# One half of the second layer's input weights stays on chip between the token tiles; the weights' ring has three places instead of four, the gathered rows' ring eight instead of ten

## The chip, the cores and the metric

The kernel runs on one core of a Trainium2 chip. The metric is the device time of one execution in microseconds (us). The median of three runs of the kernel before is 1578.97 us (1577.9 to 1581.96).

## What is computed

A decoder trunk of two layers on 256 tokens of width 1024, all in float32. Layer 0 mixes the tokens with gated linear attention, layer 1 with differential softmax attention. Each layer ends in an expert retrieval (PEER): every token picks 16 experts in each of 8 heads and takes a dot product with each expert's `u` row and a weighted sum of the `v` rows. Cut to what matters here:

```
for i in range(2):
    hn = rmsnorm(h, norm_mix[i])
    h = h + (gla_mixer if i == 0 else diff_mixer)(hn, ...)   # diff: proj = hn @ w_in (1024 x 3072), attention, @ w_out
    h = h + peer(rmsnorm(h, norm_ffn[i]), w_query[i], sub_keys[i], expert_u[i], expert_v[i])
...
def peer(...):             # per block of 128 tokens
    qry = x_blk @ w_query                                    # 1024 x 2048
    idx, gate = top 16 of the product keys, softmax          # 8 heads x 16 experts a token
    act = gelu(einsum('thkd,td->thk', expert_u[idx], x_blk))
    return einsum('thk,thkd->td', gate * act, expert_v[idx])
```

## The kernel before

**Tiles and rows.** The 256 tokens are two tiles of 128 (one token a partition). Each layer and tile has 128 expert slots, so there are 4 x 128 = 512 "rows" in all, numbered n = 0 to 511: rows 0 to 255 belong to layer 0, 256 to 383 to layer 1's first tile, 384 to 511 to its second. A row is one indirect DMA from POOL's queue: for each of the 128 partitions, the `u` and `v` vector of one expert, 8 KB a partition, 1 MB in all. DVE takes the dot product with `u` (`dot`), ACT makes gelu, weight and a 128x128 diagonal matrix of the weights (`expert_weight`), and PE multiplies that matrix with `v` into PSUM (`expert_sum`, two 128x512 products, four MATMUL records a row). PE's last product of a row counts up `v_used`. Eleven of the early rows are summed by DVE instead.

**The ring of gathered rows.** A gathered row lands in one of several places of 8 KB a partition. From row 128 on these are the ten of `LATE`; row n waits until row n - 10 is summed (`v_used`). So at any moment the ten places are split between rows on their way and rows that have landed and are not yet summed.

**Ticks.** The rest of the work (queries, attention, searches) is laid between the rows by hand: each engine's program calls `at(t)`, which emits the row work up to tick t, one row a tick. On PE the products of layer 1 (`block1`, `query1`) stand between the sums of the rows; all of it is one stream in a fixed order.

**Layer 1 for one tile** (`layer1(m)`, m = 0 and 1, starting at ticks 134 and 262): six blocks of the input projection (`block1`), attention in eight heads (`diff`), two blocks of the output projection (`block1`), four blocks of the PEER query (`query1`). While layer 1 of a tile is worked, the rows of the tile before are summed.

**The weights' ring.** The weights of these 12 blocks (2 MB each) come as 24 halves of 1 MB for each tile, in order: halves 0 to 11 are `diff_in`, 12 to 15 `diff_out`, 16 to 23 the query's. They are loaded by SP's queue into four places `A_HALF`; half n waits until half n - 4 is used. `block1` uses its two halves one after the other and counts up `half_used` after each. `query1` is different: it needs both halves at its start, since each group of 128 outputs runs over all eight k, and it counts both as used at its end:

```
for j in range(2):
    pe.wait_ge(S(f"half_loaded{(halves + j) % 4}"), 16 * ((halves + j) // 4 + 1))
for g in range(4):
    for k in range(KD):
        at(t + Q_STEP * (KD * g + k + 1))
...
last.then_inc(S("half_used"), 2)
```

The wait stands ahead of the first `at`, so every row sum that follows in PE's program stands behind it.

Of the kernel before, what the change touches and what calls it, by code (L numbers as in the profile page):

```python
# [18 lines left out]
P = 128  # L19
D = 1024  # L20
KD = D // P
SEQ = 256
NT = SEQ // P
# [64 lines left out]
WBLK = KD * 512  # L88
# [6 lines left out]
A_PA = A_TI  # L95

A_HALF = (0, 2048, 16384, 18432)
A_GAIN, A_DV, A_KT, A_KEYT1, A_FINAL = 22528, 26624, 28672, 30720, 30720

ROW = 2 * D  # L100
FIRST = ("spare", "raw0", "raw1", 6144, 4096)
EARLY = ("work0", "work1", "spare", "raw0", "raw1", 6144, 4096, "work2", "work3")
LATE = (8192, 10240, 12288, 14336, 20480, "spare", "raw0", "raw1", 6144, 4096)


def homes():

    home, turn, before, last, used = [], [], [], {}, {}
    for n in range(ROWS):
# [4 lines left out]
        else:  # L114
            at = LATE[(n - SLOTS) % len(LATE)]
        home.append(at)
# [6 lines left out]
HOME, TURNS, BEFORE = homes()  # L123
ADDED = [n for n in range(16, 80, 6)]
SUMMED = [n for n in range(ROWS) if n not in ADDED]


def summed_to(n):
    return sum(k <= n for k in SUMMED)

# [6 lines left out]
def trunk_kernel(nc, x, x_t, gains_t, positions, norm_ffn, norm_final,  # L137
# [7 lines left out]
    with ctx:  # L145
        def sb(name, shape, dt=f32):
            return ctx.enter_context(nc.sbuf_tensor(name, shape, dt))
# [3 lines left out]
        def S(name):  # L151

            if name not in sems:
                sems[name] = ctx.enter_context(nc.semaphore(name))
            return sems[name]
# [19 lines left out]
        spare = sb("spare", [P, ROW])  # L175
        bank_all = ctx.enter_context(nc.psum_tensor("banks", [P, 8 * BANK], f32))

        def bank(b, n=1):
            return bank_all[:, b * BANK:(b + n) * BANK]

        def ar(off, n):
            return arena[:, off:off + n]
# [13 lines left out]
        def x1(unit, off=0, n=D):  # L196

            return work[:, unit * D + off:unit * D + off + n]
# [35 lines left out]
        @block.sync  # L234
        def _(sp):
            for m in range(NT):
                sp.dma_start(h[:, m, :], x[0, m * P:(m + 1) * P, :]).then_inc(S(f"x{m}_loaded"), 16)
            sp.dma_start(hnT[:].rearrange("p m k t -> p (m k t)"), x_t).then_inc(S("xt_loaded"), 16)
            for half, loaded in ((0, "win_top_loaded"), (1, "win_bottom_loaded")):
                c0 = half * WBLK // 2  # L240
                sp.dma_start(ar(c0, WBLK // 2), gla_in[0][:, c0:c0 + WBLK // 2]).then_inc(S(loaded), 16)
            for j, lq in enumerate((lq1, lk1, lq2, lk2)):
                sp.dma_start(rt[:, 256 + 64 * j:256 + 64 * j + DDH], lq.broadcast_to([P, DDH])
                             ).then_inc(S("lam_loaded"), 16)

            sp.wait_ge(S("gate_done"), 1)
            sp.dma_start(hrows[:, 1, :], norm_ffn[0].rearrange("(a n) -> a n", a=1).broadcast_to([P, D])
                         ).then_inc(S("gffn_loaded"), 16)
            sp.dma_start(ar(A_KEYT, HP * P), peer_keys_t[0]).then_inc(S("keys_loaded"), 16)
            for blk in range(4):  # L250
                sp.wait_ge(S(("v_done", "r_done")[blk // 2]), NT + blk % 2 + 1)
                sp.dma_start(ar(A_WQ + blk * WBLK, WBLK), peer_query[0, blk]).then_inc(S(f"wq_loaded{blk}"), 16)

            sp.wait_ge(S("scores_done"), 4 * NT)
            sp.dma_start(ar(A_KEYT1, HP * P), peer_keys_t[1]).then_inc(S("keys1_loaded"), 16)
            sp.dma_start(ar(A_GAIN, D), norm_ffn[1].rearrange("(a n) -> a n", a=1).broadcast_to([P, D])
                         ).then_inc(S("gffn1_loaded"), 16)

            def load_halves(m, first, w, blocks):

                for j in range(2 * blocks):
                    n = 24 * m + first + j
                    if n == 0:
                        sp.wait_ge(S("listed"), NT * LISTS)
                    elif n > 3:
                        sp.wait_ge(S("half_used"), n - 3)
                    c0 = j % 2 * WBLK // 2
                    sp.dma_start(ar(A_HALF[n % 4], WBLK // 2), w[j // 2][:, c0:c0 + WBLK // 2]
                                 ).then_inc(S(f"half_loaded{n % 4}"), 16)

            for m in range(NT):
                load_halves(m, 0, diff_in, 6)
                load_halves(m, 12, diff_out, 2)
                load_halves(m, 16, peer_query[1], 4)

            sp.wait_ge(S("ffn1_rows"), NT)
            sp.dma_start(ar(A_GAIN, D), norm_final.rearrange("(a n) -> a n", a=1).broadcast_to([P, D])
                         ).then_inc(S("gfinal_loaded"), 16)
            sp.wait_ge(S("out_ready"), 1)
            sp.dma_start(out[0, 0:P, :], ar(A_FINAL, D)).then_inc(S("out_stored"), 16)  # L280
            sp.wait_ge(S("out_ready"), 2)
            sp.dma_start(out[0, P:2 * P, 0:512], ar(A_FINAL + D, 512)).then_inc(S("out_stored"), 16)
            sp.wait_ge(S("out_stored"), 16 * 2)
            sp.wait_ge(S("last_stored"), 16)
# [61 lines left out]
        def _(pe):  # L346
# [196 lines left out]
            def at(t):  # L543

                nonlocal summed
                while summed < ROWS and SUM_T[summed] < int(t):
                    if summed not in ADDED:
                        expert_sum(summed)
                    summed += 1

            halves = 0

            def block1(t, dst):

                nonlocal halves
                for k in range(KD):
                    at(t + IN_STEP * (k + 1))
                    if k % (KD // 2) == 0:
                        pe.wait_ge(S(f"half_loaded{halves % 4}"), 16 * (halves // 4 + 1))
                    last = nc.tensor.matmul(dst, x1(X_T, k * P, P),  # L560
                                            ar(A_HALF[halves % 4] + k % (KD // 2) * 512, 512),
                                            start=(k == 0), stop=(k == KD - 1))
                    if k % (KD // 2) == KD // 2 - 1:
                        last.then_inc(S("half_used"), 1)
                        halves += 1
# [55 lines left out]
            def layer1(m):  # L621
# [9 lines left out]
                for b in range(6):  # L631
                    if b == 4:
                        at(t + IN_END[3])
                        pe.wait_ge(S("rope_ready"), 2 * m + 1)
                        turn(x1(X_Q), 6, "q_turned")
                    if b > 3:
                        pe.wait_ge(S("in1_evicted"), 6 * m + b - 1)
                    block1(t + IN_END[b] - KD * IN_STEP, bank((6, 7, 4, 5, 4, 5)[b]))
# [13 lines left out]
                for b in range(2):  # L652
                    block1(t + OUT_END[b] - KD * IN_STEP, bank(4 + b))
# [5 lines left out]
                for b in range(4):  # L659
                    query1(m, b, t + Q_END[b] - 4 * KD * Q_STEP)  # L660
# [3 lines left out]
            def scores1(m, b):  # L664
                pe.wait_ge(S("keys1_loaded"), 16)
                pe.wait_ge(S("qry1_evicted"), 4 * m + b + 1)
                for g in range(4 * b, 4 * b + 4):
                    last = nc.tensor.matmul(bank(4 + b)[:, g % 4 * P:(g % 4 + 1) * P], x1(X_QRY, g * P, P),
                                            ar(A_KEYT1 + g * P, P), start=True, stop=True)
                last.then_inc(S("scores1_done"), 1)  # L670

            def query1(m, b, t):

                nonlocal halves
                for j in range(2):
                    pe.wait_ge(S(f"half_loaded{(halves + j) % 4}"), 16 * ((halves + j) // 4 + 1))
                for g in range(4):
                    for k in range(KD):
                        at(t + Q_STEP * (KD * g + k + 1))
                        w = A_HALF[(halves + k // (KD // 2)) % 4] + k % (KD // 2) * 512 + g * P  # L680
                        last = nc.tensor.matmul(bank(4 + b)[:, g * P:(g + 1) * P], ar(w, P), x1(X_T, k * P, P),  # L681
                                                start=(k == 0), stop=(k == KD - 1))
                    if g == 0 and b:
                        scores1(m, b - 1)
                last.then_inc(S("half_used"), 2)
                halves += 2
# [1042 lines left out]
```

## Time and profile before

| | us |
|---|---|
| median of three runs | 1578.97 |
| the profiled execution | 1579.55 |
| its span | 1577.5 |
| PE busy | 1362.1 (86%) |
| DVE busy | 975.1 (62%) |
| ACT busy | 670.4 (42%) |
| POOL busy | 580.3 (37%) |
| moved by DMA | 620.42 MB, mean 393 GB/s |

The time of an execution lies some 2 us over its span. The lines of a page name an engine, a source line of the kernel and the operation; PE's busy time is modelled and includes pipelined matmuls, DMA has its own share and rate. Times on the trace's axis count from the span's start.

### The profile page before, as it was taken

Reading aid. Unit: us, or ns where it says so; the run is one execution under the profiler, and the core shown is the slowest. Engines: PE = TensorE matmul, PEld = TensorE weight load, DVE = VectorE, ACT = ScalarE, POOL = GpSimd, SP = SyncE. Lnnn points to the kernel's source line nnn. Section 1 sums busy time; section 2 is a strip of 40 time slices with the busy share of each in tenths; the row PEclk is TensorE's granted clock in tenths of the full one; section 3 lists DMA queues with packets and bytes.
Section 4 is the critical chain, followed back from the end, with each engine's and each line's share of the span. In section 5 each row is a group of like instructions: output and inputs, shape, how many; then the busy total and the mean of one; then the engine's idle time right before and its main releaser. Section 6 shows DMA issues by size and latency. Waiting matters only on the chain.

```text
span 1577.5 us, 15019 instructions
## 1 busy us (share of the span) xinstructions
PE 1362.1 (86%) x4096; PEld 656.8 (42%) x4096; DVE 975.1 (62%) x2432; ACT 670.4 (42%) x1914; POOL 580.3 (37%) x532
## 2 busy tenths in 40 slices
PE   7999998889877988889989699888999877787776
PEld 5555565444323433334555244334465422222222
DVE  3327598988774344764477765566556888554544
ACT  2324443434334334873434333586433434443433
POOL 1001565554443333443433234334434433333330
PEclk9999999999998999999999799999999999999999
DMA  9317999999999999999999999999999999999995
GB/s 380 146 54 293 396 413 421 421 421 421 421 421 422 421 421 421 421 421 421 421 421 421 372 422 421 421 413 399 421 421 420 421 421 421 422 422 422 421 421 230
DMA packets 85234, 620.42 MB, mean 393 GB/s; under 512 B 10368, under 2 KB 10368, under 8 KB 11424
## 3 DMA queue, kind: packets, MB, share of 16 engines
q0 software_dynamic: 74768, 551.65, 84.4%
q1 hardware_dynamic: 9792, 67.51, 10.5%
q8 instruction: 34, 0.56, 0.1%
q10 hardware_dynamic: 592, 0.31, 0.1%
q14 instruction: 48, 0.39, 0.1%
HBM read 618.38 MB, written 1.05 MB: 393 GB/s over the span
## 4 chain that ended last, share of the span: by engine, by line
PE 40%; DMA 37%; DVE 9%; ACT 9%; issue 4%; POOL 1%; SPq 0%; ACTq 0%; DVEq 0%; POOLq 0%
PE banks L533 25%; DMA arena<-in_peer_uv_dram,hnT 24%; PE banks L560 6%; PE banks L413 5%; DMA work<-in_peer_uv_dram,hnT 5%; DMA raw<-in_peer_uv_dram,hnT 4%; DVE arena L1413 3%; DMA rt<-in_diff_lambda_k_dram 2%; ACT g_e L917 2%; PE banks L681 2%; DMA spare<-in_peer_uv_dram,hnT 2%; ACT L954 1%; PE banks L505 1%; ACT hnT L909 1%; DVE raw L1413 1%
## 5 line engine op out<-in xcount | busy, mean ns | idle before, releaser
L533 PE MATMUL banks<-arena,g_e 128*128 128x512 f32 x1184 | 585.1, 622 | 116.1 <-ACT g_e L917 115.0
L339 POOL DMA_INDIRECT arena<-in_peer_uv_dram,hnT x299 | 326.3, 1091 | 515.8 <-PE banks L533 497.8
L533 PEld LDWEIGHTS banks<-arena,g_e 128*128 128x128 f32 x1184 | 214.3, 195 | 405.5 <-ACT g_e L917 213.2
L906 ACT ACTIVATE hnT<-hnT 128x1 f32<-128x1 f32 x512 | 103.3, 202 | 631.5 <-DVE hnT L1413 629.6
L1413 DVE CUSTOM_DVE_ANT_0 arena<-arena,hrows 128x1024 f32<-128x1024 f32 x209 | 254.2, 1223 | 170.2 <-DMA arena<-in_peer_uv_dram,hnT 168.9
L533 PE MATMUL banks<-raw,g_e 128*128 128x512 f32 x424 | 205.5, 611 | 27.8 <-ACT g_e L917 25.3
L917 ACT ACTIVATE g_e<-ident,hnT 128x128 f32<-128x128 f32 x501 | 201.2, 402 | 46.5 <-ACT hnT L909 0.7
L339 POOL DMA_INDIRECT raw<-in_peer_uv_dram,hnT x106 | 118.3, 1116 | 154.1 <-PE banks L533 149.5
L909 ACT ACTIVATE hnT<-hnT,arena 128x1 f32<-128x1 f32 x512 | 150.7, 294 | 52.1 <-DVE arena L1594 5.5
L1413 DVE CUSTOM_DVE_ANT_0 arena<-arena,banks 128x1024 f32<-128x1024 f32 x90 | 109.7, 1220 | 87.3 <-DMA arena<-in_peer_uv_dram,hnT 87.2
L1413 DVE CUSTOM_DVE_ANT_0 raw<-raw,hrows 128x1024 f32<-128x1024 f32 x80 | 97.6, 1224 | 57.2 <-DMA raw<-in_peer_uv_dram,hnT 56.3
L339 POOL DMA_INDIRECT spare<-in_peer_uv_dram,hnT x53 | 56.7, 1071 | 206.6 <-DVE hnT L1582 116.2
L533 PEld LDWEIGHTS banks<-raw,g_e 128*128 128x128 f32 x424 | 75.1, 192 | 123.8 <-issue 67.9
L560 PE MATMUL banks<-arena,work 128*128 128x512 f32 x256 | 124.1, 593 | 2.5 <-ACT work L939 2.5
L533 PE MATMUL banks<-work,g_e 128*128 128x512 f32 x200 | 98.8, 620 | 18.3 <-ACT g_e L917 16.3
L533 PE MATMUL banks<-spare,g_e 128*128 128x512 f32 x196 | 98.0, 624 | 9.6 <-ACT g_e L917 9.5
L339 POOL DMA_INDIRECT work<-in_peer_uv_dram,hnT x54 | 72.7, 1347 | 81.6 <-PE banks L533 41.6
L681 PEld LDWEIGHTS banks<-work,arena 128*128 128x128 f32 x512 | 70.1, 192 | 37.9 <-issue 37.9
L1413 DVE CUSTOM_DVE_ANT_0 work<-work,hrows 128x1024 f32<-128x1024 f32 x54 | 65.7, 1221 | 24.4 <-DMA work<-in_peer_uv_dram,hnT 23.4
L505 PEld LDWEIGHTS banks<-arena 128*128 128x128 f32 x448 | 61.9, 191 | 34.9 <-issue 34.9
L560 PEld LDWEIGHTS banks<-arena,work 128*128 128x128 f32 x256 | 48.5, 190 | 64.4 <-issue 60.3
L681 PE MATMUL banks<-work,arena 128*128 128x128 f32 x512 | 70.7, 275 | 0.0
(244 smaller groups left out, 1259.2 us busy)
## 6 DMA issues: line engine op xcount, KB each, us to landing
arena<-in_diff_in_dram SPq DMA_DIRECT2D x24, 1024.0 KB
arena<-in_peer_query_dram SPq DMA_DIRECT2D x16, 1024.0 KB
arena<-in_gla_in_dram POOLq DMA_DIRECT2D x5, 2048.0 KB, 20.3
arena<-in_peer_query_dram SPq DMA_DIRECT2D x4, 2048.0 KB, 10.9
arena<-in_diff_out_dram SPq DMA_DIRECT2D x8, 1024.0 KB
arena<-in_peer_uv_dram,hnT POOLq DMA_INDIRECT x299
work<-in_gla_out_dram POOLq DMA_DIRECT2D x2, 2048.0 KB, 40.0
arena<-in_gla_in_dram SPq DMA_DIRECT2D x2, 1024.0 KB, 12.3
```

What stands on the lines that cost most here:

```text
L339: pool.indirect_dma_start(pair(n), None, table, bass.IndirectOffsetOnAxis(ap=places[:, o:o + 1].bitcast(u32), axis=0)).then_inc(S(f"pair_l ...
L413: last = nc.tensor.matmul(dst, hnT[:, m, k, :], w[:, k * 512:(k + 1) * 512], start=(k == 0), stop=(k == KD - 1))
L505: last = nc.tensor.matmul(dst[:, g * P:(g + 1) * P], ar(A_WQ + b * WBLK + k * 512 + g * P, P), ar(A_HN + m * D + k * P, P), start=(k == 0) ...
L533: last = nc.tensor.matmul(bank(2 * (tile % NT) + half), diags[:, slot * P:(slot + 1) * P], v_row(n)[:, half * 512:(half + 1) * 512], start ...
L560: last = nc.tensor.matmul(dst, x1(X_T, k * P, P), ar(A_HALF[halves % 4] + k % (KD // 2) * 512, 512), start=(k == 0), stop=(k == KD - 1))
L681: last = nc.tensor.matmul(bank(4 + b)[:, g * P:(g + 1) * P], ar(w, P), x1(X_T, k * P, P), start=(k == 0), stop=(k == KD - 1))
L906: A(acts[:, o:o + 1], dots[:, o:o + 1], ACT.Gelu).then_inc(S("gelu_done"), 1)
L909: A(weights[:, o:o + 1], acts[:, o:o + 1], ACT.Copy, scale=ar(A_GG + o, 1)).then_inc(S("weighted"), 1)
L917: A(diags[:, turn % DIAGS * P:(turn % DIAGS + 1) * P], ident[:], ACT.Copy, scale=weights[:, o:o + 1]).then_inc(S("diag_ready"), 1)
L954: last = A(x1(X_P, n % 2 * 512 + half * 256, w), x1(X_S, n % 2 * 512 + half * 256, w), ACT.Exp, bias=stat[:, 52 + (n % 2) * 2 + half:53 + ...
L1413: V.tensor_tensor_reduce(out=u_row(n), in0=u_row(n), in1=normed, scale=1.0, scalar=0.0, op0=ALU.mult, op1=ALU.add, accum_out=dots[:, o:o + ...
```

## The change

Half 5 of each tile's 24 (the second half of the third input block) gets a place of its own, 18432, the former fourth place of the ring. It is loaded in the first tile and not again in the second. All other halves go round three places: 0, 2048 and 16384. `RING` lists them; a half waits for the one three before it in that list. `LATE` loses two of its ten places, 14336 and 20480; nothing else in layer 1 takes them. No instruction of PE, DVE or ACT is added, removed or moved.

```diff
+KEPT = {5: 18432}
+HALVES = 24
+RING = [n for n in range(NT * HALVES) if n % HALVES not in KEPT]
...
-LATE = (8192, 10240, 12288, 14336, 20480, "spare", "raw0", "raw1", 6144, 4096)
+LATE = (8192, 10240, 12288, "spare", "raw0", "raw1", 6144, 4096)
...
+def half_at(n):
+
+    if n % HALVES in KEPT:
+        return KEPT[n % HALVES]
+    return A_HALF[RING.index(n) % 3]
+
+
+def half_turn(n):
+
+    return 0 if n % HALVES in KEPT else RING.index(n) // 3
...
-                    n = 24 * m + first + j
+                    n = HALVES * m + first + j
                     if n == 0:
                         sp.wait_ge(S("listed"), NT * LISTS)
-                    elif n > 3:
-                        sp.wait_ge(S("half_used"), n - 3)
+                    if n % HALVES in KEPT and m:
+                        continue
+                    if n in RING[3:]:
+                        sp.wait_ge(S("half_used"), RING[RING.index(n) - 3] + 1)
                     c0 = j % 2 * WBLK // 2
-                    sp.dma_start(ar(A_HALF[n % 4], WBLK // 2), w[j // 2][:, c0:c0 + WBLK // 2]
-                                 ).then_inc(S(f"half_loaded{n % 4}"), 16)
+                    sp.dma_start(ar(half_at(n), WBLK // 2), w[j // 2][:, c0:c0 + WBLK // 2]
+                                 ).then_inc(S(f"half_loaded_{half_at(n)}"), 16)
...
                 for j in range(2):
-                    pe.wait_ge(S(f"half_loaded{(halves + j) % 4}"), 16 * ((halves + j) // 4 + 1))
+                    pe.wait_ge(S(f"half_loaded_{half_at(halves + j)}"), 16 * (half_turn(halves + j) + 1))
```

On SP's queue, the loads of the halves stood so before (the row's number of repeats is behind the x, what it waits for in brackets):

```order
L268 DMA arena<-in_diff_in_dram 128x2048 [waits listed]
L268 DMA arena<-in_diff_in_dram 128x2048 x3
L268 DMA arena<-in_diff_in_dram 128x2048 [waits half_used] x8
L268 DMA arena<-in_diff_out_dram 128x2048 [waits half_used] x4
L268 DMA arena<-in_peer_query_dram 128x2048 [waits half_used] x8
L268 DMA arena<-in_diff_in_dram 128x2048 [waits half_used] x12
```

and stand so now, at another line number:

```order
L285 DMA arena<-in_diff_in_dram 128x2048 [waits listed]
L285 DMA arena<-in_diff_in_dram 128x2048 x2
L285 DMA arena<-in_diff_in_dram 128x2048 [waits half_used] x2
L285 DMA arena<-in_diff_in_dram 128x2048
L285 DMA arena<-in_diff_in_dram 128x2048 [waits half_used] x6
L285 DMA arena<-in_diff_out_dram 128x2048 [waits half_used] x4
L285 DMA arena<-in_peer_query_dram 128x2048 [waits half_used] x8
L285 DMA arena<-in_diff_in_dram 128x2048 [waits half_used] x11
```

Three halves instead of four go out at once at the start, half 5 follows half 4 without a wait, and the second tile loads 11 halves of `diff_in` instead of 12. On POOL's queue, the gathers from row 127 on stood so before:

```order
L339 DMA arena<-in_peer_uv_dram,hnT 128x2048 [waits v_used]
L339 DMA arena<-in_peer_uv_dram,hnT 128x2048 [waits scores_done,listed]
L339 DMA arena<-in_peer_uv_dram,hnT 128x2048 x4
L339 DMA spare<-in_peer_uv_dram,hnT 128x2048 [waits v_used]
L339 DMA raw<-in_peer_uv_dram,hnT 128x2048 [waits v_used] x2
L339 DMA arena<-in_peer_uv_dram,hnT 128x2048 [waits v_used] x7
```

and stand so now:

```order
L356 DMA arena<-in_peer_uv_dram,hnT 128x2048 [waits v_used]
L356 DMA arena<-in_peer_uv_dram,hnT 128x2048 [waits scores_done,listed]
L356 DMA arena<-in_peer_uv_dram,hnT 128x2048 x2
L356 DMA spare<-in_peer_uv_dram,hnT 128x2048 [waits v_used]
L356 DMA raw<-in_peer_uv_dram,hnT 128x2048 [waits v_used] x2
L356 DMA arena<-in_peer_uv_dram,hnT 128x2048 [waits v_used] x5
```

A round of the ring is `spare`, two of `raw` and, now, five of `arena` instead of seven.

## Rows read from the trace of the kernel before

**Rows 1.** The page: DMA's share and rate in 40 slices of 39.4 us

```profile
DMA  9317999999999999999999999999999999999995
GB/s 380 146 54 293 396 413 421 421 421 421 421 421 422 421 421 421 421 421 421 421 421 421 372 422 421 421 413 399 421 421 420 421 421 421 422 422 422 421 421 230
```

**Rows 2.** Who waited for whom, 1250 to 1550 us, POOL: total, times, longest

```profile
POOL arena L339 <- PE banks L533: 132.1, 83, 7.9
POOL raw L339 <- PE banks L533: 37.6, 24, 3.6
```

**Rows 3.** Gathers issued (L339) from 0 to a time, xcount

```profile
0.00:748.80 748.80, 273.56 (x224) 0.98 0.91 377
0.00:890.00 890.00, 320.20 (x268) 0.97 0.93 383
0.00:1140.00 1140.00, 416.56 (x352) 0.97 0.94 389
0.00:1240.00 1240.00, 458.61 (x390) 0.97 0.95 392
```

**Rows 4.** DVE's records of dot products (L1413), two a row, from 0 to a time

```profile
0.00:748.80 748.80, 264.76 (x432) 0.98 0.91 377
0.00:890.00 890.00, 321.45 (x524) 0.97 0.93 383
0.00:1140.00 1140.00, 424.12 (x694) 0.97 0.94 389
0.00:1240.00 1240.00, 467.27 (x764) 0.97 0.95 392
```

**Rows 5.** Windows: us, PE, PEld, DVE, ACT, POOL busy (xcount), PEclk, DMA share, GB/s

```profile
748.80:773.40 24.60, 23.38 (x102) 14.37 (x101) 12.79 (x23) 11.53 (x33) 10.99 (x11) 1.00 1.02 422
774.90:801.60 26.70, 24.33 (x111) 15.26 (x110) 16.67 (x54) 8.69 (x28) 8.69 (x10) 1.00 1.01 421
801.60:830.30 28.70, 24.61 (x110) 15.24 (x109) 18.97 (x45) 9.06 (x29) 10.34 (x10) 1.00 1.01 422
831.90:861.20 29.30, 26.27 (x110) 15.98 (x109) 20.69 (x66) 12.31 (x33) 9.15 (x10) 0.94 1.01 421
1164.10:1187.80 23.70, 23.70 (x111) 15.05 (x110) 14.75 (x54) 7.86 (x27) 8.71 (x10) 1.00 1.01 420
1187.80:1215.10 27.30, 24.23 (x109) 14.97 (x108) 17.39 (x42) 8.96 (x28) 9.94 (x9) 1.00 1.02 422
1216.90:1241.10 24.20, 23.90 (x110) 15.11 (x109) 20.61 (x66) 12.20 (x33) 11.37 (x11) 1.00 1.01 421
```

**Rows 6.** SP's issues in order of time around the end of a query block

```profile
773.42 29.02 SPq L268 DMA_DIRECT2D arena<-in_peer_query_dram  x4
```

**Rows 7.** SP's issue of one half at 719.23, and DMA queues 719.2 to 728.2

```profile
719.23 0.33 SPq L268 DMA_DIRECT2D arena<-in_peer_query_dram  x1
q1 hardware_dynamic: 144, 1.05, 28.0%
```

**Rows 8.** A load of 1 MB at the program's start: KB, us to landing

```profile
hnT<-in_x_t_dram SPq DMA_DIRECT2D x1, 1024.0 KB, 7.2
```

**Rows 9.** POOL's gathers in order of time, 875 to 900 us, idle before in brackets

```profile
875.80 1.66 POOL L339 DMA_INDIRECT arena<-in_peer_uv_dram,hnT  x1 [4.67 <-PE banks L533]
890.16 0.94 POOL L339 DMA_INDIRECT arena<-in_peer_uv_dram,hnT  x1 [12.71 <-PE banks L533]
```

**Rows 10.** Windows of 5 us at the drain, columns as in rows 5

```profile
885.00:890.00 5.00, 3.89 (x6) 1.71 (x7) 5.00 (x23) 2.56 (x9) 0.00 (x0) 0.50 0.85 354
890.00:895.00 5.00, 5.00 (x17) 2.94 (x16) 5.00 (x20) 3.29 (x13) 1.88 (x2) 0.90 0.72 261
```

**Rows 11.** PE in order of time at the same place

```profile
886.11 3.78 PE L533 MATMUL banks<-arena,g_e 128*128 128x512 f32 x4 [10.58 <-ACT g_e L917]
```

**Rows 12.** Windows around the second tile's attention, columns as in rows 5

```profile
1060.00:1085.00 25.00, 20.38 (x61) 9.26 (x59) 15.30 (x40) 21.60 (x65) 12.76 (x12) 1.00 0.96 372
1085.00:1140.00 55.00, 50.46 (x122) 23.11 (x123) 28.89 (x54) 24.14 (x75) 20.89 (x18) 0.94 1.01 422
```

More of the change, by code:

```diff
@@ L558, in block1 @@
                     if k % (KD // 2) == 0:
-                        pe.wait_ge(S(f"half_loaded{halves % 4}"), 16 * (halves // 4 + 1))
+                        pe.wait_ge(S(f"half_loaded_{half_at(halves)}"), 16 * (half_turn(halves) + 1))
                     last = nc.tensor.matmul(dst, x1(X_T, k * P, P),
-                                            ar(A_HALF[halves % 4] + k % (KD // 2) * 512, 512),
+                                            ar(half_at(halves) + k % (KD // 2) * 512, 512),
                                             start=(k == 0), stop=(k == KD - 1))
@@ L679, in query1 @@
                         at(t + Q_STEP * (KD * g + k + 1))
-                        w = A_HALF[(halves + k // (KD // 2)) % 4] + k % (KD // 2) * 512 + g * P
+                        w = half_at(halves + k // (KD // 2)) + k % (KD // 2) * 512 + g * P
                         last = nc.tensor.matmul(bank(4 + b)[:, g * P:(g + 1) * P], ar(w, P), x1(X_T, k * P, P),
```

## The prediction

> **What bounds the kernel now.** I read DMA's rate over the span first. From the sixth of the 40 slices on it is 421 GB/s in nearly every one [rows 1]. The dips are slice 23 (372) and slices 27 and 28 (413, 399). A rate that stays at one number while the work around it changes is a ceiling, so from about 200 us on the kernel lives at DMA's pace: a row or a half is 1.049 MB, and 1.049 MB at 421 GB/s is 2.49 us. Next, the waits of POOL, which issues the gathers. It waits for PE's sums nearly always (83 waits, 132.1 us, for the `arena` places alone in 300 us [rows 2]). That doesn't mean that PE is the bound: it means that the ring is always full, of rows on their way or landed. How they divide is what counts. Gathers issued less rows dotted (half of DVE's records) gives the rows on their way, with those landed and waiting for DVE: at 748.8 us 224 - 216 = 8, at 890 us 268 - 262 = 6, at 1140 us 352 - 347 = 5, at 1240 us 390 - 382 = 8 [rows 3, 4]. At 5 the rate is still 422 [rows 12]; where it dips (261 at 890 to 895 [rows 10], 372 at 1060 to 1085 [rows 12]) the reserve is gone. Four to five rows on their way fill the queues, so ten places hold a reserve of three to four rows in quiet stretches, none at 890, and hardly any at 1140. Last, PE in the query blocks. Where it lags (1164.1 to 1187.8) it is busy 23.70 us of 23.7 while DMA also runs at 420; the first tile's blocks are longer and have gaps [rows 5]. PE is thus the second bound, close behind.
>
> **What is taken away.** One load of 1 MB in the second tile, between 890 and 1000 us, where DMA is at its ceiling: -2.5 us.
>
> **The gathers' ring, eight places.** Row n now waits for row n - 8, so two rows fewer are on their way at each moment. In quiet stretches 8 become 6 and nothing is lost. Where the reserve runs out, DMA idles up to two rows longer, 2 x 2.49 = 5.0 us each time; the floor is 0. Three places come in question. (a) At 875 to 890 us POOL waits 12.71 us [rows 9] and the rate falls to 261 [rows 10]: no reserve is left, so I take the whole 5.0. (b) Before 725 us, in the first tile's attention, the rate holds at 421 through those slices [rows 1]; I take 1, of 0 to 5. (c) At 1060 to 1085 DMA idles already, but the engines are behind it, and PE is at 50.46 of 55.00 us in what follows [rows 12]. Rows that land later are not missed by an engine that is itself late: 0, of 0 to 5.
>
> **The weights' ring, three places.** Follow the half that a block waits for. `block1` uses a half each 8 us or so, and a half is now sent for when the third before it is used, two halves of time ahead (about 16 us); a load takes 9 (below), so these blocks don't wait. `query1` frees two halves together, at its end. In the first tile the query's halves are 16 to 23. In `RING`, half 19 waits for half 16, and 16 is freed only when query block 0 ends. But block 1 needs 18 and 19 before its first product. With four places half 19 waited for half 15, long done. So after block 0 PE stands until half 19 has been asked for and has landed. Half 20 goes out beside it; half 21 waits for 18, so block 2 waits the same way, and with half 23 block 3 too. Three stalls a tile, six in all. The kept half doesn't help: it is an input half, and far from here.
>
> How long is one? SP issues at the block's end (773.42, with its partner [rows 6]; the four issues of that row fall into two pairs, 28 us apart). A single half that was issued at 719.23 beside the gathers had its 1.05 MB moved, with the small writes that report it, by 728.2 [rows 7]: 9.0 us. At the program's start, with no gathers, 1 MB took 7.2 [rows 8]. So 7.2 to about 10, and I take 9.0, since the gathers are there. The Trainium skill says in "DMA: Bandwidth & Descriptors", section "Queues, rings and completion order", that each DMA engine takes turns between the queues that have work; by that rule a half gets half of the rate, 1.049 MB at 210 GB/s is an estimated 5 us of transfer, and what is left of the 9.0 is start and report. The trace agrees, and shows no way for the half to overtake.
>
> Behind the wait stand all of PE's row sums, so no place is freed meanwhile: POOL waits, ACT waits for the key scores of the block before, and DVE runs on with what has landed. What matters is whether PE makes good. A block's work for PE is at most 23.7 us (the row in which it was busy throughout), where the ones before took 26.7, 28.7 and 29.3 in the first tile and 23.7, 27.3 and 24.2 in the second [rows 5].
> - First tile: 3 x 9.0 = 27.0 of stall; spare 3.0 + 5.0 + 5.6 = 13.6; left 13.4. The ring enters with 8 - 2 = 6 on their way, a reserve of 1.5 rows over 4.5, 3.7 us: DMA loses 9.7.
> - Second tile: 27.0 less 0 + 3.6 + 0.5 = 4.1 leaves 22.9. Here the ring enters with no reserve. But before, the ring refilled to 8 by 1240; now it ends at 4.5 of 8 instead of 6, which DMA has kept working by 1.5 rows, 3.7 us. It loses 19.2.
> After 1240 there is only row work, DMA-bound, and what DMA lost isn't given back.
>
> **Sum.** -2.5 + 5.0 + 1 + 0 + 9.7 + 19.2 = +32.4 us. On the profiled execution's 1579.55 that is 1612; it lies 0.6 over the median, so I say 1612 and 2.1% slower.
>
> **Rivals.**
> - *The stalls are mostly covered* (0.18). The reserve of the ring and the gaps in PE take them, as a half is faster when the gathers run dry (7.2 each: 43.2 us less 17.7 of spare, less 7.4 of reserve: 18.1), and the second tile's blocks turn out to have more slack than their busy time tells. With the drain, 1583 to 1599. For it: PE's busy time is modelled. Against it: the row of 23.70 of 23.7 with DMA at 420.
> - *PE also comes back at a lower clock* (0.14). After the wait of 10.58 us PE's first four products took 3.78 us at a granted clock of 0.50 and the next window shows 0.90, one of its 5 us still low [rows 10, 11]; 0.50 is the lower of the two levels, 1.2 GHz. From 886.1 to 891 is 4.9 us, which at half speed costs 2.5; six times 2.5 is 15 more: 1620 to 1640. Against it: that low clock began in a stretch where PE had been idling between rows. "TensorE: Matmul & The Clock Gate" of the Trainium skill, section "HAM oscillation", says that a matmul loop which waits for its weights each time comes back cold each time. The trace has one such wait and it agrees; none lies in a busy query block.
> - *Not slower* (0.08): only the byte count matters, -2.5 us, 1577. It needs each stall and drain to be under the reserve: six rows on their way must outlast 9 us of standing PE, which two landed rows and a half use up once but not three times. It decides if a half is there within some 4 us of its issue.
> - *The change saves more than its bytes* (0.02), as SP's and POOL's traffic mingle less; no row speaks for it.
> - My forecast, stalls exposed at full clock (0.58): 1600 to 1626 as its own range.
>
> **How the numbers follow.** The own range and the two slow rivals reach from 1583 to 1640. Cutting the rare ends leaves 1588 to 1630, about 8 in 10. Within 0.3% (4.7 us, about what a measurement of this kernel can tell) is 1574.3 to 1583.7: the not-slower rival and the lowest edge of the covered one, 0.09. Faster 0.02, slower 0.89.
>
> **What would show it.** In the trace after: PE idle for 8 to 10 us at the starts of query blocks 1, 2 and 3 of each tile, ended by the landing of a half, six places in all, and none in `block1`. DMA's rate under 421 in the slices of both query stages (it was 421 in the first before), and deeper dips at 890. 1 MB less moved (619.4 MB). From the last query block to the end the same 2.49 us a row as before. Gathers issued less rows dotted at 6 in quiet stretches, where it was 8. It is wrong if PE's waits for the halves are short (then the load is faster than I read it), if they are there and DMA stays at 421 (then the reserve was larger), or if the rate falls in quiet stretches too (then six rows on their way don't fill the queues, and the time is beyond my range).

## The result and the profile after

The changed kernel takes 1614.56 us (median of 4, 1609.6 to 1616.25), the kernel before 1578.72. The ratio is 1.0222, 95% interval 1.0208 to 1.0236: 2.2% slower, 35 us. The profiled execution took 1616.25 us, its span is 1614.3, the span before was 1577.5. To compare runs of different calls, every difference below is a kernel's ratio to the kernel before that ran beside it, times 1578.7 us.

From the page of the changed kernel, PE's granted clock in 40 slices of 40.4 us, DMA's share and rate in the same slices, and what it moved:

```profile
PEclk9999999999998999999888999989988899999999
DMA  9317999999999999999988999999998899999996
GB/s 383 131 52 293 396 422 420 421 421 422 420 421 405 422 421 421 413 419 422 387 334 353 418 421 421 418 352 417 421 400 324 343 423 420 422 421 422 421 422 264
DMA packets 85090, 619.37 MB, mean 384 GB/s; under 512 B 10352, under 2 KB 10352, under 8 KB 11408
```

Where the kernel before held 421 [rows 1], there are now two valleys: slices 20 to 22 (387, 334, 353) and slices 30 to 32 (400, 324, 343). They are the two query stages. The granted clock reads 8 in just these six slices and in slices 13 and 27, 9 in all others. Slice 27, in the second tile's attention, is deeper than any was there before (352, where the lowest was 399), and at the first tile's end, where before slice 23 read 372, no dip is left: it reads 418 now. After slice 32 the rate is 421 again.

PE in order of time at the six places (start, us busy, line, operation, in brackets the idle time before and what ended it):

```profile
782.63 3.69 PE L550 MATMUL banks<-arena,g_e 128*128 128x512 f32 x4 [9.15 <-issue]
...
787.05 1.88 PE L550 MATMUL banks<-arena,g_e 128*128 128x512 f32 x4
...
819.18 1.20 PE L698 MATMUL banks<-work,arena 128*128 128x128 f32 x4 [9.38 <-DMA arena<-in_peer_query_dram]
...
854.65 2.90 PE L550 MATMUL banks<-spare,g_e 128*128 128x512 f32 x3 [9.54 <-issue]
...
1183.62 3.75 PE L550 MATMUL banks<-arena,g_e 128*128 128x512 f32 x4 [9.20 <-issue]
...
1221.80 1.19 PE L698 MATMUL banks<-work,arena 128*128 128x128 f32 x4 [10.15 <-DMA arena<-in_peer_query_dram]
...
1257.09 1.19 PE L550 MATMUL banks<-spare,g_e 128*128 128x512 f32 x1 [9.28 <-issue]
```

Leaving out the row at 787.05, these are the six stalls, 9.15 to 10.15 us, at the starts of query blocks 1, 2 and 3 of each tile. Two of the rows name the landing of the query's weights. The other four say "issue": the first instruction behind the wait is there a row sum (L550), which waits for nothing itself. I read them as the same wait: it stands alone ahead of an instruction, and what was late is known from the program's order. A row's four products took 3.69 us right after the first stall, and 1.88 at 787.05, which is the usual.

How POOL felt one of them, after the second stall:

```profile
824.07 1.62 POOL L356 DMA_INDIRECT arena<-in_peer_uv_dram,hnT  x1 [13.49 <-PE banks L550]
826.46 0.94 POOL L356 DMA_INDIRECT spare<-in_peer_uv_dram,hnT  x1 [0.77 <-PE banks L550]
```

Gathers issued (L356) from the start to a time, xcount:

```profile
0.00:749.50 749.50, 260.25 (x222) 0.98 0.91 374
0.00:824.00 824.00, 281.79 (x242) 0.97 0.91 375
0.00:1174.40 1174.40, 413.85 (x360) 0.96 0.93 382
```

and DVE's records of dot products (L1430), two a row:

```profile
0.00:749.50 749.50, 264.44 (x432) 0.98 0.91 374
0.00:824.00 824.00, 295.58 (x483) 0.97 0.91 375
0.00:1174.40 1174.40, 433.12 (x708) 0.96 0.93 382
```

On their way are 222 - 216 = 6 at 749.5, where it was 8 [rows 3, 4]; 242 - 241.5, at most one, at 824.0, just before POOL issues again behind the second stall; and 360 - 354 = 6 at 1174.4, where the second tile's stalls begin.

Windows over the changed kernel (us, PE, PEld, DVE, ACT and POOL busy with counts, granted clock, DMA share, GB/s):

```profile
740.00:885.00 145.00, 113.11 (x469) 68.11 (x468) 83.76 (x222) 50.98 (x151) 48.47 (x44) 0.89 0.93 369
885.00:1140.00 255.00, 228.31 (x582) 101.41 (x581) 158.67 (x392) 129.55 (x364) 96.13 (x85) 0.96 0.99 408
1140.00:1300.00 160.00, 126.16 (x491) 73.67 (x490) 89.57 (x237) 56.87 (x166) 49.82 (x49) 0.89 0.93 372
1300.00:1560.00 260.00, 208.17 (x422) 73.99 (x422) 158.58 (x348) 106.54 (x329) 99.22 (x106) 0.98 1.01 421
```

A stretch at r GB/s loses its length times (1 - r/421). That is 145 x 52/421 = 17.9 us in the first query stage and 160 x 49/421 = 18.6 in the second, 36.5 together. The query stages of the kernel before lost nothing in all its seven block windows (420 to 422 [rows 5]). The time is in these two stages. A window's rate is rounded to 1 GB/s, which is 0.3 to 0.6 us of loss in windows of this length.

### The profile page after: what moved, and what is told of

It is laid out like the page before. It is cut to its first block, busy times and chain, and to the rows that moved or that the text cites. A ratio compares the mean times of both kernels' runs of the same rounds, so it can differ in the third digit from the quotient of the medians.

```text
span 1614.3 us, 15018 instructions
## 1 busy us (share of the span) xinstructions
PE 1365.5 (85%) x4096; PEld 661.4 (41%) x4096; DVE 974.3 (60%) x2432; ACT 669.2 (41%) x1914; POOL 567.3 (35%) x532
## 4 chain that ended last, share of the span: by engine, by line
PE 45%; DMA 29%; DVE 10%; ACT 8%; issue 6%; POOL 0%; SPq 0%; ACTq 0%; DVEq 0%; POOLq 0%
PE banks L550 29%; DMA raw<-in_peer_uv_dram,hnT 11%; DMA arena<-in_peer_uv_dram,hnT 7%; PE banks L430 5%; DMA work<-in_peer_uv_dram,hnT 5%; PE banks L577 5%; PE banks L698 3%; DMA spare<-in_peer_uv_dram,hnT 3%; DMA rt<-in_diff_lambda_k_dram 2%; ACT g_e L934 2%; DVE arena L1430 2%; DVE raw L1430 1%; DMA arena<-in_peer_query_dram 1%; PE banks L522 1%; ACT L971 1%
## 5 line engine op out<-in xcount | busy, mean ns | idle before, releaser
L550 PE MATMUL banks<-arena,g_e 128*128 128x512 f32 x1064 | 526.2, 623 | 91.2 <-ACT g_e L934 70.6
L356 POOL DMA_INDIRECT arena<-in_peer_uv_dram,hnT x269 | 289.1, 1075 | 465.3 <-PE banks L550 448.8
L550 PEld LDWEIGHTS banks<-arena,g_e 128*128 128x128 f32 x1064 | 193.1, 195 | 346.5 <-issue 193.0
L1430 DVE CUSTOM_DVE_ANT_0 arena<-arena,hrows 128x1024 f32<-128x1024 f32 x189 | 230.0, 1223 | 159.7 <-DMA arena<-in_peer_uv_dram,hnT 159.7
L550 PE MATMUL banks<-raw,g_e 128*128 128x512 f32 x504 | 252.6, 628 | 40.7 <-ACT g_e L934 40.4
L356 POOL DMA_INDIRECT raw<-in_peer_uv_dram,hnT x126 | 134.4, 1067 | 213.5 <-PE banks L550 210.5
L1430 DVE CUSTOM_DVE_ANT_0 raw<-raw,hrows 128x1024 f32<-128x1024 f32 x94 | 114.8, 1223 | 75.8 <-DMA raw<-in_peer_uv_dram,hnT 75.7
L550 PEld LDWEIGHTS banks<-raw,g_e 128*128 128x128 f32 x504 | 91.5, 197 | 158.0 <-ACT g_e L934 80.3
L356 POOL DMA_INDIRECT spare<-in_peer_uv_dram,hnT x63 | 66.2, 1051 | 248.8 <-PE banks L550 119.3
L1430 DVE CUSTOM_DVE_ANT_0 arena<-arena,banks 128x1024 f32<-128x1024 f32 x80 | 97.3, 1219 | 78.5 <-DMA arena<-in_peer_uv_dram,hnT 69.4
L550 PE MATMUL banks<-spare,g_e 128*128 128x512 f32 x236 | 117.0, 619 | 32.5 <-issue 18.8
L550 PE MATMUL banks<-work,g_e 128*128 128x512 f32 x200 | 97.1, 612 | 19.0 <-ACT g_e L934 18.6
L356 POOL DMA_INDIRECT work<-in_peer_uv_dram,hnT x54 | 71.3, 1321 | 85.1 <-PE banks L550 43.4
L698 PE MATMUL banks<-work,arena 128*128 128x128 f32 x512 | 73.1, 280 | 19.5 <-DMA arena<-in_peer_query_dram 19.5
L1430 DVE CUSTOM_DVE_ANT_0 spare<-spare,hrows 128x1024 f32<-128x1024 f32 x47 | 57.4, 1222 | 47.4 <-DMA spare<-in_peer_uv_dram,hnT 47.4
L950 ACT ACTIVATE work<-banks 128x512 f32<-128x512 f32 (+3 forms) x44 | 23.2, 528 | 142.1 <-PE banks L685 94.2
L1430 DVE CUSTOM_DVE_ANT_0 work<-work,hrows 128x1024 f32<-128x1024 f32 x54 | 65.6, 1219 | 25.9 <-DMA work<-in_peer_uv_dram,hnT 25.9
```

Source lines behind the costliest of these rows:

```text
L356: pool.indirect_dma_start(pair(n), None, table, bass.IndirectOffsetOnAxis(ap=places[:, o:o + 1].bitcast(u32), axis=0)).then_inc(S(f"pair_l ...
L550: last = nc.tensor.matmul(bank(2 * (tile % NT) + half), diags[:, slot * P:(slot + 1) * P], v_row(n)[:, half * 512:(half + 1) * 512], start ...
L950: A(dst, src, ACT.Copy, scale=scale).then_inc(S(done), 1)
L1430: V.tensor_tensor_reduce(out=u_row(n), in0=u_row(n), in1=normed, scale=1.0, scalar=0.0, op0=ALU.mult, op1=ALU.add, accum_out=dots[:, o:o + ...
```

## The experiments

Ten kernels ran. All but the second are edits of the changed kernel, shown against it.

**1. Ten places for the gathers again.**

```diff
-LATE = (8192, 10240, 12288, "spare", "raw0", "raw1", 6144, 4096)
+LATE = (8192, 10240, 12288, 14336, 20480, "spare", "raw0", "raw1", 6144, 4096)
```

> The changed kernel with the gathers' ring put back to ten places; the weights' ring keeps three places and half 5 stays kept. My theory (the six stalls of PE in the query blocks cost most of it): the stalls are still there at 9 to 10 us each, the ring's reserve of some 3.5 rows (8.7 us) takes a part of them in each tile, and the drains at the tile's end and in the second attention go: 1593 to 1603 us. Rival (the eight places are the cause, and the stalls are covered): within 5 us of the kernel before, 1574 to 1582.

Measured: 1602.7 us, ratio 1.0165 (1.0146 to 1.0185), +26 us. The rival falls. The stalls stand (9.0 to 9.9 us, six), and even ten places don't cover them. The time lies at the upper edge of what I expected: the reserve of ten places buys less than I had thought.

**2. Eight places alone**, in the kernel before.

```diff
-LATE = (8192, 10240, 12288, 14336, 20480, "spare", "raw0", "raw1", 6144, 4096)
+LATE = (8192, 10240, 12288, "spare", "raw0", "raw1", 6144, 4096)
```

> The kernel before with eight places for the gathers instead of ten and nothing else: four halves in the weights' ring, none kept. Written after the kernel that keeps half 19 had come within 0.1% of the kernel before. My theory as predicted: two drains, 5 and 1 us, 1582 to 1587. Rival (eight places are the cause of the whole loss): 1610 to 1620. What the kernel with half 19 suggests: it has two stalls and saves 2.5 us, and is 1.4 us slower, so eight places can cost no more than some 4 us: 1579 to 1582.

Measured: 1583.81 us, ratio 1.0035 (1.0023 to 1.0047), +5.5 us. The rate over the 40 slices:

```profile
GB/s 381 144 53 293 396 418 421 421 421 421 421 421 417 417 421 421 421 408 420 421 421 421 355 421 422 421 398 393 421 421 420 421 421 421 422 421 421 421 422 259
```

The end of the first tile (355, was 372) and its attention (398, 393, were 413, 399 [rows 1]) dip deeper, and slices 13, 14 and 18 dip for the first time (417, 417, 408, were 422, 421, 421); quiet stretches stay at 421. Six rows on their way fill the queues.

**3. The kept half's worth:** eight places, half 5 kept, four places for the weights.

```diff
-A_HALF = (0, 2048, 16384, 18432)
+A_HALF = (0, 2048, 16384, 14336)
...
-    return A_HALF[RING.index(n) % 3]
+    return A_HALF[RING.index(n) % 4]
...
-                    if n in RING[3:]:
-                        sp.wait_ge(S("half_used"), RING[RING.index(n) - 3] + 1)
+                    if n in RING[4:]:
+                        sp.wait_ge(S("half_used"), RING[RING.index(n) - 4] + 1)
```

> The changed kernel with a fourth place for the weights' ring (14336, which the change leaves empty): half 5 kept, eight places for the gathers. It differs from the kernel before with eight places only in the kept half, so the difference of the two is what a load of 1 MB less is worth. If DMA is the bound where the load falls away: 2 to 3 us faster than that kernel. If the engines are the bound there: the same.

Measured: 1580.99 us, ratio 1.0017 (1.0008 to 1.0026), +2.7 us. Beside experiment 2 on the same chip that is 2.8 us less for one load less, where 1.049 MB at 421 GB/s is 2.49. And the changed kernel differs from this one in the fourth place of the ring alone: 35.0 - 2.7 = 32.3 us are the price of the six stalls.

**4. Another half kept:** one stall a tile instead of three.

```diff
-KEPT = {5: 18432}
+KEPT = {19: 18432}
```

> The changed kernel with another half kept: half 19 (the second half of query block 1) instead of half 5. Bytes, places and program order are the same as in the changed kernel. By the rule of the ring of three, block 1 then finds both halves, block 2's two are both sent for after block 0, and only block 3 still waits: two stalls of PE instead of six. My theory: 1588 to 1600 us, with PE idle over 8 us in two query blocks. Rival (ring of eight): as the changed kernel, 1610 to 1618.

Measured: 1579.98 us, ratio 1.0011 (1.0002 to 1.0021), +1.7 us: below what I expected. PE in order of time at its two stalls:

```profile
836.27 3.75 PE L550 MATMUL banks<-spare,g_e 128*128 128x512 f32 x4 [9.21 <-issue]
...
1219.78 2.90 PE L550 MATMUL banks<-spare,g_e 128*128 128x512 f32 x3 [9.07 <-DMA arena<-in_peer_query_dram]
```

They are as long as the others, and the clock is low behind them too (0.50 from 835 to 840, 0.58 from 1220 to 1225). Yet this kernel, with the same bytes and the same eight places as experiment 3, is no slower than it (+1.7 against +2.7). A tile's one stall is free.

In the first tile that isn't the ring's reserve alone. From 740 to 930 us, which takes in the query stage and the tile's end, experiment 3 and this kernel read:

```profile
740.00:930.00 190.00, 163.77 (x585) 90.27 (x586) 125.02 (x339) 73.86 (x221) 67.60 (x60) 0.94 0.99 409
...
740.00:930.00 190.00, 169.31 (x600) 93.26 (x600) 126.19 (x352) 73.44 (x221) 68.99 (x63) 0.95 1.00 413
```

That is 190 x 12/421 = 5.4 us lost without a stall and 190 x 8/421 = 3.6 with one. In experiment 3 the loss comes at the tile's end (294, 335 and 407 GB/s in the three windows of 10 us from 880 on); here the stall's loss comes at 840 to 860 (342, 356), and the tile's end runs at 420 to 421. The stall takes the place of a drain that this ring has anyway. In the second tile the stall costs 160 x 5/421 = 1.9 us.

**5. Two stalls a tile.**

```diff
-KEPT = {5: 18432}
+KEPT = {17: 18432}
```

> The changed kernel with half 17 kept instead of half 5: same bytes, places and order. By the ring's rule query block 1 finds its halves, blocks 2 and 3 wait: two stalls a tile, where the changed kernel has three and the one that keeps half 19 has one. If every stall costs the same, the six of the changed kernel being worth some 34 us: four cost 22, so 1602 to 1605. If a tile's first stall is covered by the ring's reserve and the later ones are not, which is what the kernel with half 19 suggests (its two cost nothing that shows): 1588 to 1599.

Measured: 1593.06 us, ratio 1.0087 (1.0073 to 1.01), +13.7 us, 11.0 over experiment 3. So two, four and six stalls cost about 0, 11 and 32 us: not a price for each, but nothing for the first pair, 11 for the second and 21 for the third.

**6. PE kept busy while it waits.** The extra products are not part of the computation.

```diff
                 for j in range(2):
+                    if j and b:
+                        for _ in range(10):
+                            nc.tensor.matmul(bank(4 + b), x1(X_T, 0, P), ar(half_at(halves), 512),
+                                             start=True, stop=True)
                     pe.wait_ge(S(f"half_loaded_{half_at(halves + j)}"), 16 * (half_turn(halves + j) + 1))
```

> The changed kernel with ten extra products of 128x512 (0.86 us each, results overwritten) on PE ahead of the wait for the second half of query blocks 1 to 3, so that PE is busy while it would stand. Nothing else changes; the extra products are not part of the computation. If the lower clock after each stall costs some 2 us a stall (it was low for 3.2 to 5.3 us after PE's return in five of six), this kernel is faster than the changed one by 6 to 12 us, 1602 to 1608, and its granted clock stays up in both query stages. If the clock costs nothing on the path, it is the same or up to 3 us slower, 1613 to 1618.

Measured: 1597.27 us, ratio 1.0122 (1.0105 to 1.0139), +19.3 us: 15.7 us faster than the changed kernel by doing more, and faster than the 1602 to 1608 that I had expected. Its windows over the two query stages:

```profile
740.00:885.00 145.00, 139.09 (x540) 79.10 (x540) 86.50 (x227) 51.59 (x153) 49.94 (x46) 1.00 0.97 387
...
1140.00:1300.00 160.00, 155.15 (x562) 83.07 (x561) 102.91 (x292) 58.27 (x180) 57.82 (x56) 1.00 0.97 395
```

The clock is 1.00, where it was 0.89, and the loss of DMA is 145 x 34/421 = 11.7 and 160 x 26/421 = 9.9 us instead of 17.9 and 18.6. The filled waits are as long as the real ones. The first:

```profile
769.87 8.75 PE L695 MATMUL banks<-arena,work 128*128 128x512 f32 x20
779.16 1.13 PE L550 MATMUL banks<-arena,g_e 128*128 128x512 f32 x2 [0.54 <-DMA arena<-in_peer_query_dram]
```

From 769.87 to 779.16 is 9.3 us, and the six are 9.1 to 9.95, 55.9 in all, where the changed kernel's are 56.7. What differs is PE's work behind them: from the end of one stall to the start of the next it takes 25.9 to 28.0 us in the changed kernel and 23.6 to 25.3 here, 1.9 to 2.7 less each time. So of the 32.3 us nearly half is PE's lower clock after each stall. The windows of the changed kernel around the first stall show it:

```profile
770.00:775.00 5.00, 3.48 (x17) 2.09 (x16) 2.95 (x8) 2.28 (x7) 1.87 (x2) 1.00 1.01 419
775.00:780.00 5.00, 0.00 (x0) 0.00 (x0) 1.90 (x4) 1.80 (x6) 0.00 (x0) 0.59 1.01 421
780.00:785.00 5.00, 2.37 (x3) 1.17 (x4) 1.23 (x2) 0.00 (x0) 0.00 (x0) 0.50 1.02 423
785.00:790.00 5.00, 5.00 (x22) 2.98 (x21) 0.00 (x0) 0.00 (x0) 1.73 (x2) 0.89 0.90 334
```

While PE stands the clock falls to 0.50, that is 1.2 GHz, and the first products behind the wait run at it. The Trainium skill names this in "TensorE: Matmul & The Clock Gate", section "HAM oscillation": a loop that waits for its weights comes back cold each time. The trace agrees, six times of six.

**7. Sums ahead of the wait.** The memory and the bytes of the changed kernel; the wait stands behind three ticks of row sums.

```diff
+                lead = 3 if b else 0
+                if b:
+                    at(t + Q_STEP * KD)
+                    scores1(m, b - 1)
+                    at(t + lead)
                 for j in range(2):
                     pe.wait_ge(S(f"half_loaded_{half_at(halves + j)}"), 16 * (half_turn(halves + j) + 1))
                 for g in range(4):
                     for k in range(KD):
-                        at(t + Q_STEP * (KD * g + k + 1))
+                        at(t + lead + (Q_STEP - lead / (4 * KD)) * (KD * g + k + 1))
...
-                    if g == 0 and b:
-                        scores1(m, b - 1)
```

> The changed kernel with the wait of query blocks 1 to 3 moved behind the row sums of the block's first three ticks and the key scores of the block before; the block's products are packed into the rest of its ticks. Memory and bytes stay as in the changed kernel. My theory: PE sums the landed rows while the half is on its way, a stall shrinks from 9 to 10 us to 3 to 6, places are freed and the ring doesn't drain: 1590 to 1604 us. Rival (ring of eight is the cause): 1611 to 1617. If the rows summed there have not landed, PE waits for them instead and little is won: 1606 to 1612.

Measured: 1582.07 us, ratio 1.0021 (1.001 to 1.0032), +3.3 us, far better than I expected. PE's waits (total us, times, longest):

```profile
PE banks L703 <- DMA arena<-in_peer_query_dram: 12.8, 4, 3.8
```

The loads are as late as before. The line names four of the six waits; the other two show as issue again, at 840.66 (3.42 us) and 1225.31 (3.23), so what is left is 19.5 us in six, where it was 56.7. A late load is harmless if something useful stands ahead of the wait: each summed row frees a place, and POOL goes on. In both windows of the query stages (740 to 885, 1140 to 1300) the rate is 421. The loss came less from the late half itself than from what stood behind the wait.

**8. The same memory as before, half 5 kept:** four places for the weights, nine for the gathers.

```diff
-LATE = (8192, 10240, 12288, "spare", "raw0", "raw1", 6144, 4096)
+LATE = (8192, 10240, 12288, 20480, "spare", "raw0", "raw1", 6144, 4096)
...
-A_HALF = (0, 2048, 16384, 18432)
+A_HALF = (0, 2048, 16384, 14336)
```

(and the ring of four as in experiment 3)

> Half 5 kept, four places for the weights' ring and nine for the gathers: the same memory as the kernel before. Known by now: eight places alone cost 5.6 us, the kept half saves 2.8. Theory: the ninth place takes back more than half of the 5.6, so 1576 to 1579. Rival (only ten places are enough): 1580 to 1582.

Measured: 1577.61 us, ratio 0.9995 (0.9986 to 1.0004): no difference from the kernel before.

**9. The same memory, halves 19 and 23 kept:** three places for the weights, nine for the gathers.

```diff
-KEPT = {5: 18432}
+KEPT = {19: 18432, 23: 14336}
...
-LATE = (8192, 10240, 12288, "spare", "raw0", "raw1", 6144, 4096)
+LATE = (8192, 10240, 12288, 20480, "spare", "raw0", "raw1", 6144, 4096)
```

> Halves 19 and 23 kept in the places 18432 and 14336, three places for the weights' ring, nine for the gathers: the same memory as the kernel before. By the ring's rule no query block waits: half 20 and 21 are sent for after block 0, half 22 after block 1. Theory (bytes count once no stall is left): two loads less are 5.0 us, one place less costs up to 1: 1573 to 1576, faster than both kernels. Rival (a saved load is worth nothing, as PE and DMA are both near their bounds): 1577 to 1580.

Measured: 1574.69 us, ratio 0.9975 (0.9966 to 0.9984), 3.9 us faster than the kernel before, and faster than both. Its page shows 618.32 MB moved. With these two halves out of the way the ring of three has each query half in flight in time: from 740 to 1300 us the trace has no wait of PE for one.

**10. Three halves kept:** three places for the weights, eight for the gathers.

```diff
-KEPT = {5: 18432}
+KEPT = {5: 20480, 19: 18432, 23: 14336}
```

> Halves 5, 19 and 23 kept, three places for the weights' ring, eight for the gathers: the same memory as the kernel before, every place used. Theory (bytes count): three loads less are 7.5 us, two places less cost 1 to 4: 1572 to 1576. Rival (places of the gathers are worth more than loads): slower than the kernel that keeps two.

Measured: 1575.88 us, ratio 0.9985 (0.9976 to 0.9994). One load less and one place less than experiment 9: 1.5 us slower by the ratios, whose intervals overlap. No gain is shown there.

## Why the prediction was right, and where not

The time came out 2.2% slower where I had said 2.1%. The mechanism is shown step by step: the six stalls are in the trace at the places named, a fourth place for the ring takes them away (experiment 3), and so does the choice of the kept half in part (4 and 5). But several terms of the sum were wrong, and they nearly cancelled; that the time fits to 3 us is in that part luck.

- **What is taken away:** -2.5, measured -2.8. Right.
- **The gathers' ring:** 5.0 + 1 + 0 = 6.0, measured 5.5. The sum is right, its parts aren't. By the slices of experiment 2 against rows 1 the first tile's end loses 17/421 of 39.4 us, 1.6, where I had 5.0; slices 13, 14 and 18, before 725 us, lose 2.1 where I had 1; the second tile's attention loses 2.0 where I had 0. In the changed kernel the first of the three isn't there at all: from 890 to 910 us its rate is 423. I had forecast a deeper dip there.
- **The length of a stall:** 9.0, measured 9.15 to 10.15. Right.
- **First tile's stalls:** 9.7. With the clock kept up the first tile loses 11.7 us, and nothing more at its end, where experiment 3 loses 5.4 in a drain (below). The stalls' own price is 6.3, 3.4 less than I had.
- **Second tile's stalls:** 19.2, measured 9.9 with the clock kept up. Wrong by a factor of two. The delay of PE was near: blocks 1 to 3 took 1264.6 - 1162.3 = 102.3 us in the filled kernel and 1241.1 - 1162.6 = 78.5 before, 23.8 more, where I had 22.9. The step that failed is what I took off for the ring, "here the ring enters with no reserve" and 3.7 us for the way it ends: 13.9 us were covered.
- **The lower clock:** I counted nothing, and gave it 0.14 as a rival with 15 us. Measured 15.7 (experiment 6 against the changed kernel, with waits of the same length). The rival was right in mechanism and size, though not in its 1620 to 1640, which stood on the other terms. The argument against it, that low clocks had come only after thin stretches, weighed a lack of cases as if it were evidence.

Where the 13.9 us come from is in the counts at the start and the end of these three blocks. Gathers issued and DVE's records of dot products, first of the kernel before, then of the filled one:

```profile
0.00:1162.60 1162.60, 426.11 (x361) 0.97 0.95 390
0.00:1241.10 1241.10, 458.77 (x391) 0.97 0.95 392
0.00:1162.60 1162.60, 435.21 (x712) 0.97 0.95 390
0.00:1241.10 1241.10, 468.31 (x765) 0.97 0.95 392
...
0.00:1162.30 1162.30, 413.80 (x360) 0.98 0.94 385
0.00:1264.60 1264.60, 443.68 (x389) 0.98 0.94 385
0.00:1162.30 1162.30, 432.43 (x707) 0.98 0.94 385
0.00:1264.60 1264.60, 469.86 (x768) 0.98 0.94 385
```

Before, the rows on their way grow from 361 - 356 = 5 to 391 - 382.5 = 8.5; in the filled kernel they shrink from 360 - 353.5 = 6.5 to 389 - 384 = 5. (It issues one gather fewer there and one half of the weights more, which cancel.) So DMA moves five rows more in these blocks of the filled kernel than in those of the kernel before, and that work fills 12.5 of the 13.9 us; such counts are good to a row. I had reckoned with 1.5 rows.

I had read 5 of ten on their way at 1140 us and taken two off. Experiment 2, eight places and nothing else, shows why that is wrong. Gathers issued, dot records and PE's records of row sums up to 1162.6, and behind them the last of the kernel before:

```profile
0.00:1162.60 1162.60, 430.49 (x360) 0.97 0.94 388
0.00:1162.60 1162.60, 433.30 (x708) 0.97 0.94 388
0.00:1162.60 1162.60, 669.76 (x1365) 249.46 (x1366) 0.97 0.94 388
...
0.00:1162.60 1162.60, 668.94 (x1365) 248.46 (x1366) 0.97 0.95 390
```

PE is at the very same product in both kernels: 1365 records are 341 rows, with the eleven that DVE sums 352. The ten places hold 361 - 352 = 9 rows then, 5 on their way and 4 dotted and waiting for PE, which is late there; the eight hold 360 - 352 = 8, 6 on their way and 2 waiting. The smaller ring has fewer rows waiting for PE, not fewer on their way.

Beside experiment 3, which has the same rings but for the stalls, DMA's lost time adds up by stage. The first stage of the filled and of the changed kernel:

```profile
740.00:930.00 190.00, 181.20 (x639) 98.33 (x640) 120.61 (x329) 70.17 (x213) 65.03 (x60) 0.98 0.98 395
...
740.00:930.00 190.00, 150.98 (x558) 85.05 (x557) 116.50 (x320) 70.86 (x212) 64.82 (x58) 0.90 0.95 380
```

In each cell the rate in GB/s and the loss in us that follows from it:

| | 740 to 930 | 930 to 1140 | 1140 to 1300 | loss | over experiment 3 | time over experiment 3 |
|---|---|---|---|---|---|---|
| experiment 3 | 409, 5.4 | 410, 5.5 | 421, 0 | 10.9 | | |
| half 19 kept (4) | 413, 3.6 | 409, 6.0 | 416, 1.9 | 11.5 | 0.6 | -1.0 |
| filled (6) | 395, 11.7 | 410, 5.5 | 395, 9.9 | 27.1 | 16.2 | 16.6 |
| the changed kernel | 380, 18.5 | 406, 7.5 | 372, 18.6 | 44.6 | 33.7 | 32.3 |

The last two columns agree to 2 us. The filled kernel's loss in the query stages alone, 11.7 + 9.9, and 15.7 for the clock are 37.3, 5 us too much, because the stalls do away with the drain of 5.4 at the first tile's end. The prediction counted both, 5.0 and 9.7. The sum was right to 3 us, and its parts were up to 16 off.

That the stalls are mostly covered fell with experiment 1, which takes away the smaller ring and leaves +26 us. That ten places would buy 8.7 us a tile was wrong: 28.8 us (26.0 and the kept half's 2.8) with ten against 32.3 with eight, 3.5 in all. What the two kept-half kernels show fits: one stall in a tile is covered, two are in part, and three outrun eight places and ten alike.

## What to carry to other kernels

The depth of a ring of buffers is counted from the step that frees them to the step that needs them, not in places: here the consumer takes two halves at its start and frees both at its end, so with three places it holds two while only one load can be under way, and the half that the next block needs last is sent for only when this block ends. Which buffer is kept decides more than how many: half 5 or half 19 in the same place is 33 us of difference. Where a load must come late, put the work that frees other buffers ahead of the wait; it costs no memory.

## What the hardware showed that I had not expected

- The low clock behind a stall of PE of 9 to 10 us has a price of its own: with PE kept busy by products that nobody reads, the kernel is 15.7 us faster, 2.6 us for each of six stalls.
- Stalls don't add. Two, four and six of the same length cost about 0, 11 and 32 us beside the same kernel without them.
- The load of 1 MB took 9 to 10 us beside the gathers (the stalls of 9.15 to 10.15; the page's median from issue to landing is 9.6 for the query's halves) even when the ring of gathers was nearly dry at its end.
- The drain at a tile's end and the stalls ahead of it don't add either: with the stalls the rate at the first tile's end is 423, without them 294 and 335.
